# The second expert table read by column halves, with Pool centring one of the two output tiles

## What is computed

```python
def one_block(args):                       # PEER, 128 tokens at a time
    xb, ib, gb = args
    ug = jnp.take(u_tab, ib, axis=0)
    vg = jnp.take(v_tab, ib, axis=0)
    h = jnp.einsum('td,tkd->tk', xb, ug)
    a = (jax.nn.gelu(h.astype(jnp.float32), approximate=False) * gb).astype(xb.dtype)
    return jnp.einsum('tk,tkd->td', a, vg)
...
f = peer_layer(x, peer_wq[i], peer_keys1[i], peer_keys2[i], peer_u[i], peer_v[i])
e = jax.nn.sigmoid(x @ ple_gate_w) * (p @ ple_w)      # written short
x = layer_norm(ALPHA * x + f + e, ln2_g[i], ln2_b[i])
```

## Time and profile before

| | us |
|---|---|
| median of 3 runs | 2297.95 (2296.25 to 2298.79) |
| the profiled execution | 2300.4 |
| its span, first to last instruction | 2298.8 |
| PE busy | 2246.0 (98% of the span) |
| DVE busy | 1530.9 (67%) |
| ACT busy | 1065.5 (46%) |
| Pool busy | 46.1 (2%) |

### The profile page before, as it was taken

One profiled execution on the slowest core, in us unless ns is written; L12 is line 12 of the kernel. 1 busy time (PEld: TensorE's weight loads), 2 busy tenths in 40 slices (PEclk: granted clock), 3 DMA queues, 4 the chain that ended last, 5 costly groups with the idle time before them and its releaser, 6 DMA issues.

```text
span 2298.8 us, 39185 instructions
## 1 busy us (share of the span) xinstructions
PE 2246.0 (98%) x12096; PEld 1935.7 (84%) x12096; DVE 1530.9 (67%) x2818; ACT 1065.5 (46%) x1483; POOL 46.1 (2%) x93
## 2 busy tenths in 40 slices
PE   6999999899999999999999999999999999999996
PEld 5888888898888888888888888888888888888885
DVE  6547666665744488988888888887555555555556
ACT  3544555554444444445554444444444444444442
POOL 1000000000000000011000000000000000000000
PEclk9999999999999999999999999999999999999998
DMA  7555555457555556565545555455666666666663
GB/s 256 184 190 174 183 178 176 152 182 244 168 192 180 172 183 197 188 204 193 189 161 163 164 162 163 159 163 172 194 191 197 202 203 205 203 203 203 201 192 119
DMA packets 122728, 425.39 MB, mean 185 GB/s; under 512 B 13448, under 2 KB 21656, under 8 KB 121792
## 3 DMA queue, kind: packets, MB, share of 16 engines
q1 hardware_dynamic: 119040, 410.04, 56.0%
q0 software_dynamic: 3648, 14.82, 2.1%
HBM read 420.60 MB, written 6.31 MB: 186 GB/s over the span
## 4 chain that ended last, share of the span: by engine, by line
PE 90%; DVE 5%; issue 2%; DMA 2%; ACT 0%; DVEq 0%; SPq 0%; ACTq 0%
PE ps L1428 28%; PE ps L1446 25%; PE ps L1434 15%; PE ps L1453 12%; PE ps L1704 2%; DVE w_lo L801 1%; PE ps L1411 1%; PE ps L1416 1%; PE ps L1412 1%; DMA raw<-in_w_in 1%; PE ps L1492 1%; PE ps L1498 0%; DMA ln_gb<-in_ln_in 0%; PE ps L1574 0%; DVE bn L813 0%
## 5 line engine op out<-in xcount | busy, mean ns | idle before, releaser
L801 DVE TENSOR_TENSOR w_lo<-raw,w_hi 128x1024 fp32r<-128x1024 f32 x770 | 940.4, 1223 | 457.2 <-PE ps L1453 384.6
L488 ACT ACTIVATE w_hi<-raw 128x1024 fp32r<-128x1024 f32 x770 | 815.6, 1061 | 925.9 <-DMA raw<-in_peer_v 374.3
L1428 PE MATMUL ps<-x_t_hi_lo,w_hi 128*128 128x512 f32 x3200 | 816.0, 397 | 1.2 <-DVE experts L910 1.2
L1428 PEld LDWEIGHTS ps<-x_t_hi_lo,w_hi 128*128 128x128 f32 x3200 | 574.0, 189 | 107.1 <-issue 2.7
L1446 PE MATMUL ps<-w_hi,x_t_hi_lo 128*128 128x512 f32 x2560 | 633.2, 389 | 1.3 <-DVE x_t_hi_lo L1346 1.2
L1446 PEld LDWEIGHTS ps<-w_hi,x_t_hi_lo 128*128 128x128 f32 x2560 | 479.7, 188 | 101.1 <-issue 1.8
L1434 PEld LDWEIGHTS ps<-x_t_hi_lo,w_lo 128*128 128x128 f32 x3200 | 434.5, 190 | 39.5 <-DVE w_lo L801 8.3
L1434 PE MATMUL ps<-x_t_hi_lo,w_lo 128*128 128x256 f32 x3200 | 447.3, 282 | 2.0 <-DVE w_lo L801 1.6
L1453 PE MATMUL ps<-w_lo,x_t_hi_lo 128*128 128x512 f32 x1280 | 342.2, 389 | 0.5 <-DVE w_lo L801 0.5
L1453 PEld LDWEIGHTS ps<-w_lo,x_t_hi_lo 128*128 128x128 f32 x1280 | 240.2, 188 | 50.8 <-DVE w_lo L801 0.9
L1704 PE MATMUL ps<-onehots 128*128 128x128 f32 x512 | 77.0, 274 | 0.0
(11 more groups left out here) (213 smaller groups left out, 1136.4 us busy)
## 6 DMA issues: line engine op xcount, KB each, us to landing
raw<-in_u SPq DMA_DIRECT2D x256, 512.0 KB, 4.5
raw<-in_peer_v SPq DMA_DIRECT2D x256, 512.0 KB, 4.7
raw<-in_w_in SPq DMA_DIRECT2D x128, 512.0 KB, 4.2
raw<-in_branch SPq DMA_DIRECT2D x32, 512.0 KB, 4.6
raw<-in_wout SPq DMA_DIRECT2D x32, 512.0 KB, 4.8
raw<-in_pleg SPq DMA_DIRECT2D x32, 512.0 KB, 3.8
raw<-in_wq SPq DMA_DIRECT2D x32, 512.0 KB, 3.8
x<-in_x SPq DMA_DIRECT2D x2, 1024.0 KB, 6.3
```

The source lines that it names most:

```text
L488: nc.scalar.activation(HI[:, u % 4, :], RAW[:, u % 4, :], ACT.Copy).then_inc(hi_ready, 1)
L801: v.tensor_tensor(LO[:, u % 2, :], RAW[:, u % 4, :], HI[:, u % 4, :].bitcast(F32), ALU.subtract) \
L1428: mm(PS[:, bank, :], w(HI, u % 4)[:, k, :], XHL[:, 8 * half + k, :, :].rearrange("p a t -> p (a t)"), start=(half == 0 and k == 0), stop=F ...
```

## The change

The order of the second table's units: first all 128 chunks with the left column half (PSUM banks 0, 1, 4, 5), then all 128 with the right one (banks 2, 3, 6, 7). Each chunk of activations is now split twice, once for either half, into eight slots instead of four, and four chunks ahead instead of two. DVE adds the left half's sums to the residual and takes their `bn_stats` between the last eight units. Behind the last unit there are four adds and four `bn_stats`. Tile 1 is measured first, and Pool centres it, in four instructions of 128x1024, while DVE centres tile 0. Pool's 16 loads now run in the second half of the phase, one for every five chunks, which are five units now and were ten.

```diff
+                if name == "vtab":
+                    for half in range(2):
+                        with sp.Fori(0, NK // 4) as i:
+                            for j in range(4):
+                                load(i, 4, b + NK * half + j,
+                                     a["peer_v"][:, i * 4 + j, half * UNIT:(half + 1) * UNIT])
+                    continue
...
-            pool.wait_ge(al_ready, VT0 + 36)
+            pool.wait_ge(al_ready, VT0 + NK + 36)
...
-                pool.wait_ge(ah_ready, VT0 + 36 + 5 * piece)
+                pool.wait_ge(ah_ready, VT0 + NK + 36 + 5 * piece)
...
+            pool.wait_ge(ln_in[2], 16 * 8)
+            pool.wait_ge(mean_ready, 1)
+            for h in range(2):
+                cols = slice(h * UNIT, (h + 1) * UNIT)
+                step(nc.gpsimd.tensor_scalar(RES2[:, 1, cols], RES2[:, 1, cols], MV[:, 1, 0:1], None, ALU.subtract))
+                nc.gpsimd.tensor_tensor(RES2[:, 1, cols], RES2[:, 1, cols], LNG2[:, 0, cols], ALU.mult
+                                        ).then_inc(centred_in, 1)
...
-            def a_hi(i, c):
+            def a_hi(i, half, c):
-                act.wait_ge(unit_done, val(i, 8, vb + 2 * c - 6))
-                nc.scalar.activation(XH[:, c % 4, :], BUF[:, bass.ds(val(i, 4, c), 1), :].rearrange("p a t -> p (a t)"),
+                act.wait_ge(unit_done, val(i, 8, vb + NK * half + c - 7))
+                nc.scalar.activation(XH[:, c % 8, :], BUF[:, bass.ds(val(i, 8, c), 1), :].rearrange("p a t -> p (a t)"),
                                      ACT.Copy).then_inc(ah_ready, 1)
...
+            def vt_body(i, half, start=0):
+                for c in range(start, start + 8):
+                    conv(i, 8, vb + NK * half + c + ACT_LEAD)
+                    a_hi(i, half, c + 4)
...
+            def added2(tt, q):
+                x = RES2[:, tt, q * 512:(q + 1) * 512]
+                ch.tag(v.tensor_tensor(x, nbank(tt, q), x, ALU.add))
+
+            for half in range(2):
+                with dve.Fori(0, NK // 8 - 1) as i:
+                    for c in range(8):
+                        conv(i, 8, vb + NK * half + c + DVE_LEAD)
+                        a_lo(i, half, c + 4)
+                for c in range(NK - 8, NK):
+                    if vb + NK * half + c + DVE_LEAD < UNITS:
+                        conv(None, 8, vb + NK * half + c + DVE_LEAD)
+                    if c + 4 < NK:
+                        a_lo(None, half, c + 4)
+                    elif half == 0:
+                        a_lo(None, 1, c + 4 - NK)
+                    if half and c < NK - 4:
+                        dve.wait_ge(res_in, 16 * 8)
+                        added2(*first_cols[c - (NK - 8)])
+                    elif half:
+                        ch.wait()
+                        quarter(RES2, *first_cols[c - (NK - 4)])
...
+            dve.wait_ge(unit_done, UNITS)
+            for tt, q in last_cols:
+                added2(tt, q)
+            for tt in (1, 0):
+                ch.wait()
+                for q in (2, 3):
+                    quarter(RES2, tt, q)
+                ch.wait()
+                ins = v.bn_aggr(MV[:, tt, :], STATS[:, tt, :, :].rearrange("p a b -> p (a b)"))
+                if tt:
+                    ins.then_inc(mean_ready, 1)
+                    dve.wait_ge(mean_ready, 1)
+                else:
+                    ch.link(ins)
             variance()
             centre(RES2, LNG2, 0)
...
-            centre(RES2, LNG2, 1)
-            ch.wait()
             for half in range(2):
+                dve.wait_ge(centred_in, half + 1)
                 rescale(RES2, LNG2, 1, half, out_ready)
...
+            def vt_unit(i, half, c, first=False, last=False):
+                pe.wait_ge(al_ready, val(i, 8, VT0 + NK * half + c + 1))
+                n_unit(i, 8, vb + NK * half + c, XH[:, c % 8, :], XL[:, c % 8, :], first, last, half)
```

More of the change, by code:

```diff
@@ L778, in _ @@
                     act.wait_ge(unit_done, vb - 1)
-                    a_hi(None, 0)
+                    a_hi(None, 0, 0)
                 if j % 2:
                     gelu_chunk(B_ITERS - 1, j // 2)
-            a_hi(None, 1)
-            with act.Fori(0, 31) as i:
-                vt_body(i, 0, False)
+            for c in range(1, 4):
+                a_hi(None, 0, c)
             act.wait_ge(dve_evac, 80)
-            vt_body(None, 124, True)
+            for half in range(2):
+                with act.Fori(0, NK // 8 - 1) as i:
+                    vt_body(i, half)
+                vt_last(half)
             std_of(3)
@@ L1341, in _ @@
             vb = BASE["vtab"]
-            def a_lo(i, c):
-                dve.wait_ge(ah_ready, val(i, 4, VT0 + c + 1))
-                v.tensor_tensor(XL[:, c % 4, :], BUF[:, bass.ds(val(i, 4, c), 1), :].rearrange("p a t -> p (a t)"),
-                                XH[:, c % 4, :].bitcast(F32), ALU.subtract).then_inc(al_ready, 1)
-            def vt_body(i, c0, last):
-                for c in range(4):
-                    k = c0 + c
-                    conv(i, 8, vb + 2 * k + DVE_LEAD)
-                    if not (last and k + 2 >= NK):
-                        a_lo(i, k + 2)
-                    if not (last and k + 1 >= NK):
-                        conv(i, 8, vb + 2 * k + 1 + DVE_LEAD)
@@ L1358, in _, with a_lo @@
-            a_lo(None, 0)
+            def a_lo(i, half, c):
+                dve.wait_ge(ah_ready, val(i, 8, VT0 + NK * half + c + 1))
+                v.tensor_tensor(XL[:, c % 8, :], BUF[:, bass.ds(val(i, 8, c), 1), :].rearrange("p a t -> p (a t)"),
+                                XH[:, c % 8, :].bitcast(F32), ALU.subtract).then_inc(al_ready, 1)
+            a_lo(None, 0, 0)
             halves(None, 2 * B_ITERS - 1)
             gated(None, 2 * B_ITERS - 1)
-            a_lo(None, 1)
-            with dve.Fori(0, 31) as i:
-                vt_body(i, 0, False)
@@ L1364, in _ @@
-            vt_body(None, 124, True)
-            dve.wait_ge(res_in, 16 * 8)
-            dve.wait_ge(ln_in[2], 16 * 8)
-            for half in range(2):
-                dve.wait_ge(unit_done, UNITS - 1 + half)
-                for tt in range(NT):
-                    for q in (2 * half, 2 * half + 1):
-                        x = RES2[:, tt, q * 512:(q + 1) * 512]
-                        ch.tag(v.tensor_tensor(x, nbank(tt, q), x, ALU.add))
-            ch.wait()
-            for tt in range(NT):
-                stats(RES2, tt)
+            for c in range(1, 4):
+                a_lo(None, 0, c)
@@ L1734, in _ @@
             vb = BASE["vtab"]
-            def vt_body(i, c0, first, last):
-                for c in range(4):
-                    pe.wait_ge(al_ready, val(i, 4, VT0 + c0 + c + 1))
-                    for j in range(2):
-                        if first and c == 0 and j:
-                            pe.wait_ge(joined, U_J + NK)
-                        n_unit(i, 8, vb + 2 * (c0 + c) + j, XH[:, c, :], XL[:, c, :],
-                               first and c == 0, last and c == 3)
-            vt_body(None, 0, True, False)
-            with pe.Fori(1, 31) as i:
-                vt_body(i, 0, False, False)
-            vt_body(None, 124, False, True)
+            def vt_unit(i, half, c, first=False, last=False):
+                pe.wait_ge(al_ready, val(i, 8, VT0 + NK * half + c + 1))
+                n_unit(i, 8, vb + NK * half + c, XH[:, c % 8, :], XL[:, c % 8, :], first, last, half)
+            for half in range(2):
+                for c in range(8):
+                    vt_unit(None, half, c, first=(c == 0))
+                with pe.Fori(1, NK // 8 - 1) as i:
+                    for c in range(8):
+                        vt_unit(i, half, c)
+                for c in range(NK - 8, NK):
+                    vt_unit(None, half, c, last=(c == NK - 1))
+                if half == 0:
+                    pe.wait_ge(joined, U_J + NK)
 def kernel(**inputs):
```

23 lines of the change are left out of this document (14 added, 9 removed).

## The result

| | kernel before | changed kernel |
|---|---|---|
| median, us | 2298.03 (2295.42 to 2300.91, 13 runs) | 2303.96 (2300.71 to 2308.97, 13 runs) |
| ratio after / before | | 1.0027, 95% interval 1.0019 to 1.0035 |
| profiled execution, its span | 2300.4, 2298.8 | 2308.97, 2307.3 |
| second table, first to last matmul | 696.6 (1580.12 to 2276.70) | 706.8 (1578.45 to 2285.20) |
| PE's last matmul to DVE's last pass | 18.87 | 18.98 |

A forecast was written before the change was run, and what follows sets the result against it. PE was taken to bound the kernel, 2.72 us a unit. With 0 for its phase and -0.3 us for the end, the median 2297.95 became 2297.6 us; the overall range was 2292.8 to 2303, the forecast's own 2296.5 to 2299.

The forecast's parts named there:

- PE's own work: Second table's phase: all 256 units stay at 2.72 us with four banks and one activation wait per unit; counted 0.
- the second splitting: Second table's phase: 51 us more on ACT and 54 on DVE, hidden by busy time within 2.72 us a unit.
- The ring: Second table's phase: load, ACT and DVE passes wait in a circle of 7.98 us against 8.16 for three units; counted 0.
- The lead of 3.0 us: Second table's phase: `w_lo` is done 3.0 us before its unit needs it, so a single late load does no harm.
- Rival 2: Second table's phase: the circle through the load turns too slowly; at a mean landing of 5.0, 7.2 us slower; chance 0.20.
- Pool's loads "fit": Second half of the phase: 16 loads some 13.6 us apart fit, with DMAs busy 64%, though they lengthen single landings.
- The end as DVE alone: After PE's last matmul, Pool free of charge: 2.47 us less for statistics, 2.38 for centring, 0.1 added; gain 4.75 us.
- The end with Pool: After PE's last matmul: Pool and DVE take turns reading SBUF, leaving a gain of 0.3 us.
- The signs for the end: Profile marks after PE's last matmul: second `bn_aggr` 2.5 us earlier; tile 0's centring 1.5 us late or at once; Pool's pass length.
- Rival 1: After PE's last matmul: Pool and DVE read SBUF side by side, giving 2293.2 us, up to 2296 with partial holding; chance 0.27.

The follow-up runs named there:

- ring4_act: The changed kernel with two lines of ACT's loop swapped, so the activations' high part is issued ahead of `w_hi`; 2297.25 us, ratio 0.9996 to the kernel before.
- after_again: The changed kernel, unaltered, profiled again on another occasion beside three other kernels on one chip; 2304.04 us, one run, second-table phase 700.9 us.
- last_unit_by_tiles: ring4_dve_centres with PE finishing tile 0 before tile 1 in the very last unit; 2293.6 us, ratio 0.9987 to the kernel before.
- ring4_dve_centres: ring4_act with the centring of tile 1 taken from Pool and put back on DVE; 2296.4 us, ratio 0.9991 to the kernel before.
- pool_fills_end: ring4_act with Pool's four centring passes replaced by fills of the same size, which read nothing; 2292.09 us, one run.
- pool_alone: ring4_act with Pool centring only once both tiles are measured, and DVE waiting for all four Pool passes; 2304.04 us, one run, end 25.04 us.
- ring4_dve: The changed kernel with DVE making the rest of the activations three chunks on, not four, ACT left alone; 2298.55 us, ratio 1.0004 to the kernel before.

## Why the prediction was wrong

- **PE's own work, and the second splitting by busy time: right.** Units of 2.72 us with four banks and with one wait per unit (ring4_act), at DVE's and ACT's higher load.
- **The ring: found, and mis-sized. This is the step that failed.** "With both I count 0 for the phase": the sum was 7.98 us with a margin of 0.18. Its fixed parts, the ring's turn less the landing, measure 3.36 us (median of 248 turns in the changed kernel) and not 3.28. Its landing measures 4.90 us, not 4.7. Together 8.26 for 8.16, so the term put at 0 cost 10.2 us in this execution and 4.3 in after_again. The break-even is a landing of 4.80, not 4.88. I took the landing from a kernel with other addresses and with Pool's loads half as dense, though I had said that these lengthen landings. The outcome hangs on hundredths: in the estimate by landings above, fixed parts of 3.33 or 3.40 in place of 3.36 give a loss of 6 or 12 us.
- **The lead of 3.0 us: right, but used up.** "A single late load does no harm" holds only while the ring recovers. With a margin of nothing, latenesses add up, and single loads of 6.7 us then reach PE. Loads of 6.6 us in ring4_act and 6.9 in last_unit_by_tiles, with a ring of four, cost nothing.
- **Rival 2: this is what happened**, in its mechanism and its signs (waits of DVE put down to ACT, gaps ahead of the `w_lo` matmuls). Its price was too low, 7.2 us at a mean of 5.0 where 10.2 at 4.90 was measured (and 4.3 at 4.81): it took a mean over the whole phase, where the second half has the longer landings, took the whole lead off once, and left out that PE never gets back what a single late load takes. And the chance of 0.20 was too low for a margin of 0.18 us in 8.16 against landings that spread from 3.8 to 6.2.
- **Pool's loads "fit": right by bandwidth, wrong in effect.** With the short ring they cost some 3 us by the medians, just visible.
- **The end as DVE alone: right.** -2.47 for the statistics; ring4_dve_centres measured 16.57 against 18.87, -2.30. With both terms, -4.75 was forecast, and pool_fills_end measured 14.19, -4.68. Some 0.1 of the difference is that DVE now starts 0.11 us after PE's last matmul (2285.20 to 2285.31), and ran up to it before (2276.70 to 2276.74).
- **The end with Pool: right in the total** (a gain of 0.3 forecast, a loss of 0.1 measured) **and in the mechanism** (turns, shown by pool_alone and by the fills), **but wrong in where the turns come, so that the total is in part luck.** The forecast had DVE's centring wait 1.5 us for Pool's second pass. It started at once, since it met a one-input pass, and it was Pool's second pass that waited. The held passes were the steps for 1 / std and the third rescaling, 4.8 us in all, where the forecast's own places came to some 4.4. One size was wrong too: a one-input pass takes 2.84 us, not 1.0. It did no more harm because DVE was held for only part of it: beside the third pass the second step was held 0.9 us.
- **The signs for the end misled.** A centring that "starts at once and takes 2.35 us beside Pool" was to show rival 1; it did just that, and rival 1 is false. "A Pool pass of more than 3 us would make both wrong"; there were two, 3.14 and 3.31, and tile 1 still didn't wait for Pool alone (Pool ended at 2301.89, the last rescaling began at 2302.90). Only the second `bn_aggr` told rightly, 2.3 us earlier for 2.5.
- Rival 1 did not happen; pool_fills_end shows what it would have given, an end of 14.2 us. ring4_act and ring4_dve are what the forecast described, and lie in its own range of 2296.5 to 2299: 2297.25 and 2298.55.

The Trainium skill, "SBUF — State Buffer", section "Who interferes with whom", has the rule that a DVE instruction with two SBUF inputs contends with a GpSimd instruction that reads SBUF, not with one that only writes. The runs bear out the second half, 2.35 us for 2.35 over the fills, and the first half beside Pool's two-input passes, 3.36 us for 1.28. Beside Pool's one-input pass, which reads too, they bear it out only in part: one step was held 0.9 us, while a centring and a rescaling took their usual 2.35 and 1.28. The Trainium skill, "GPSIMD Engine Reference", section "Elementwise — side-by-side cycle accounting", gives 4497 ns for 2048 columns with two inputs, half of that an estimate of 2.25 us for 1024; the trace has 2.33.

## What to carry to other kernels

Busy time does not show whether work that is put into a queue is hidden: follow what it waits for, and add up every ring that runs through a DMA, with its landing, against the number of units it spans. If the margin is smaller than the spread of the landings, count it as lost, and look for an order that lengthens the ring by a unit; here that was one swap of two lines. And an idle engine is not free if it reads the same memory as the busy one: here four passes on Pool saved DVE 2.4 us of work and held it for 4.8.

## What the runs showed of the hardware

- Loads of the same size and shape (128 rows of 4 KB) landed about 0.2 us later in the second half of the phase when they read 8 KB apart from load to load, all left halves of the rows first and then all right ones, than when they read the two halves of a row in turn (4.62 to 4.80, 4.64 to 4.82, 4.70 to 4.90). In the first half there was no such difference. Why is not shown.
- A load of 512 KB in flight beside one of Pool's 256 KB loads landed 0.2 to 0.4 us later than the others of that stretch (4.84 for 4.60 in the kernel before, 5.10 for 4.74 in the changed one).
- Pool's `tensor_scalar` with a scalar per partition on 128x1024 float32 takes 2.84 us, longer than its `tensor_tensor` with two inputs, 2.33; a fill of that size takes 0.95.
- While such a one-input pass ran, a two-input DVE pass on 128x2 was held for about 0.9 us of its 2.83, and the rescaling after it not at all, though the pass was still running. While Pool's two-input pass ran, DVE's two-input passes were held to its end (1.98 us for 0.16, 3.36 for 1.28); a one-input DVE step, the reciprocal, took its usual 0.17.
